# A four-layer hybrid transformer on one core: two of four weight pieces of the last feed-forward go from GpSimd to ScalarE and VectorE, the delta-net's key products move between the levels of its inverse, and the norms ask for their table earlier

## The reference

```python
def layer_norm(t, g, b):
    mu = jnp.mean(tf, -1, keepdims=True)
    var = jnp.mean(jnp.square(tf - mu), -1, keepdims=True)
    return ((tf - mu) * lax.rsqrt(var + NORM_EPS)).astype(t.dtype) * g + b

def conv_glu(t, w_up, conv_w, conv_b, w_down):       # D_FF = 2816
    hdn = t @ w_up
    val, gt = hdn[..., :D_FF], hdn[..., D_FF:]
    gt = dwconv(gt, conv_w) + conv_b
    return (jax.nn.silu(gt) * val) @ w_down

# gated delta-net: 8 heads, both directions, one chunk
tmat = triangular_solve(eye + lmat, eye)             # lmat from k k^T, beta and decay
def step(s, inp):
    v_new = uu - ww @ s
    o = qd @ s + aa @ v_new
    s = s * jnp.exp(gl)[..., None, None] + jnp.einsum('bhcd,bhce->bhde', kd, v_new)
    return s, o
# finish: rms_norm of o per head, times silu(gate), times w_o
```

## Time and profile before

| | us |
|---|---|
| median of 3 runs (2896.61 to 2898.7) | 2898.62 |
| the profiled execution, own time | 2901.96 |
| its span | 2899.9 |
| TensorE busy | 2652.6 (91%) |
| GpSimd busy | 1626.6 (56%) |
| VectorE busy | 1183.2 (41%) |
| ScalarE busy | 788.1 (27%) |

### The profile page before, as it was taken

The page is one execution under the profiler, slowest core; times in us unless marked ns, Lnnn a source line. Parts: engine busy times, 40 slices in busy tenths (PEclk is TensorE's granted clock), DMA queues, the critical chain, the costliest instruction groups (busy, mean ns, idle before and its releaser), DMA issues. The chain is left out here.

```text
span 2899.9 us, 45667 instructions
## 1 busy us (share of the span) xinstructions
PE 2652.6 (91%) x16461; PEld 2132.3 (74%) x16461; DVE 1183.2 (41%) x2197; ACT 788.1 (27%) x1490; POOL 1626.6 (56%) x1665
## 2 busy tenths in 40 slices
PE   6988999999898899899999999898999998888987
PEld 4766677787687788767778668886677786767886
DVE  2364322222469667432222320674322223443455
ACT  2253322210541433132211140441322113243311
POOL 3402566665657222466667556775666575607985
PEclk8999999999899989899999999999999999999998
DMA  6333455422222000255542222002555322203442
GB/s 236 117 117 117 155 172 173 151 87 87 61 73 87 16 2 1 73 173 173 173 132 87 73 76 88 16 1 89 188 174 174 116 88 72 88 1 116 159 145 87
DMA packets 217162, 305.60 MB, mean 105 GB/s; under 512 B 7332, under 2 KB 155551, under 8 KB 217024
## 3 DMA queue, kind: packets, MB, share of 16 engines
q1 hardware_dynamic: 179007, 228.16, 23.9%
q10 hardware_dynamic: 38016, 75.50, 8.0%
HBM read 302.60 MB, written 1.05 MB: 105 GB/s over the span
## 5 line engine op out<-in xcount | busy, mean ns | idle before, releaser
L588 POOL TENSOR_TENSOR w_lo<-w_raw,w_hi 128x512 fp32r<-128x512 f32 x720 | 948.5, 1317 | 108.2 <-POOL w_hi L585 88.1
L585 POOL TENSOR_SCALAR w_hi<-w_raw 128x512 fp32r<-128x512 f32 x720 | 472.1, 656 | 871.9 <-PE bank L1055 609.4
L1055 PE MATMUL bank<-u_lo,w_hi 128*128 128x512 f32 (+1 forms) x2144 | 810.3, 378 | 43.9 <-DVE u_lo L1725 21.5
L1055 PE MATMUL bank<-u_hi,w_lo 128*128 128x512 f32 (+1 forms) x2144 | 791.7, 369 | 0.0
L1055 PE MATMUL bank<-u_hi,w_hi 128*128 128x512 f32 (+1 forms) x2144 | 791.6, 369 | 0.0
L1055 PEld LDWEIGHTS bank<-u_lo,w_hi 128*128 128x128 f32 x2144 | 408.8, 191 | 182.9 <-issue 99.3
L1055 PEld LDWEIGHTS bank<-u_hi,w_hi 128*128 128x128 f32 x2144 | 408.7, 191 | 68.5
L1055 PEld LDWEIGHTS bank<-u_hi,w_lo 128*128 128x128 f32 x2144 | 409.4, 191 | 63.0
L1633 PE MATMUL bank<-gs_lo,w_hi 128*128 128x512 f32 (+1 forms) x576 | 212.2, 368 | 9.4 <-DVE gs_lo L2339 6.1
L1633 PE MATMUL bank<-gs_hi,w_lo 128*128 128x512 f32 (+1 forms) x576 | 211.1, 366 | 0.0
L1633 PE MATMUL bank<-gs_hi,w_hi 128*128 128x512 f32 (+1 forms) x576 | 211.1, 366 | 0.0
(11 more groups left out here) (334 smaller groups left out, 3859.6 us busy)
## 6 DMA issues: line engine op xcount, KB each, us to landing
w_raw<-in_ffn_w_up SPq DMA_DIRECT2D x88, 1024.0 KB, 7.1
ada_w<-in_ada_w ACTq DMA_DIRECT2D x72, 1024.0 KB, 5.2
w_raw<-in_ffn_w_down SPq DMA_DIRECT2D x44, 1024.0 KB, 4.9
ada_w<-in_ada_w SPq DMA_DIRECT2D x16, 1024.0 KB, 5.1
w_raw<-in_gdn_w_in SPq DMA_DIRECT2D x16, 1024.0 KB, 5.7
w_raw<-in_attn_w_qkv SPq DMA_DIRECT2D x12, 1024.0 KB, 5.3
w_raw<-in_gla_w_in SPq DMA_DIRECT2D x12, 1024.0 KB, 5.3
ada<-in_ada_w SPq DMA_DIRECT2D x8, 1024.0 KB, 13.5
```

The lines of the kernel that those rows point to most:

```text
L585: eng.tensor_scalar(w_hi[:, q, :], src, 1.0, 0.0, ALU.mult, ALU.add).then_inc(pool.own, pool.step())
L588: eng.tensor_tensor(w_lo[:, q, :], src, w_hi[:, q, :].bitcast(F32), ALU.subtract).then_inc(w_split, 1)
L1055: mm = eng.matmul(bank[banks[m]][:, T], w[:, q, c:c + P], v[:, k, T], start=(k == 0 and n == 0), stop=(k == KT - 1 and n == 2))
```

## The change

Three groups of edits.

1. Last feed-forward: GpSimd splits pieces 0 and 1 of a unit. Pieces 2 and 3 are rounded by ScalarE (`upper` on ScalarE) as soon as the same piece of the unit before has been multiplied, and VectorE subtracts (`upper` on VectorE). The release of a slot waits for 2 counts of `w_split` and 2 of `w_fourth`. The calls stand in fixed places of the in-order queues: on ScalarE ahead of the convolution's centre and ahead of silu.
2. Delta-net: the product of keys and state (`key_state`) is issued for d = 0 behind the first level of the inverse and for d = 1 behind the second; VectorE's residual values move behind its copies of the second level. In the two turns with s = 3 the transposed keys, decayed keys, state products and state updates are left out, as their result is not used. Waits follow.
3. Norms and finish: the one-column Sqrt (`root_table`) moves ahead of the wait for the means, and one is added at the head of `head_finish`, whose VectorE part gates four tiles before it inverts the root, and the others between the heads.

```diff
@@ load (SyncE)
-                    eng.wait_ge(w_split, sp.next(w_split, 3 if shared else 4))
+                    eng.wait_ge(w_split, sp.next(w_split, 2 if shared else 4))
                     sp.stand()
                     if shared:
-                        eng.wait_ge(w_fourth, sp.next(w_fourth))
+                        eng.wait_ge(w_fourth, sp.next(w_fourth, 2))
@@ delta_net (GpSimd)
-                        if (s, hg) != (0, 0):
+                        if (s, hg) == (TT - 1, 1):
+                            eng.wait_ge(od_ready, 14)
+                        elif (s, hg) != (0, 0):
                             eng.wait_ge(s_done, pool.next(s_done, 2))
@@ GpSimd, layers
-                pieces = 3 if last(l) else 4
+                pieces = 2 if last(l) else 4
@@ delta_net (ScalarE)
-                eng.wait_ge(s_done, act.next(s_done, 2))
-                eng.wait_ge(st_upd, act.next(st_upd))
+                eng.wait_ge(bo_ready, 16)
@@ head_finish, norm_stats (ScalarE)
+                root_table()
                 for i, t in enumerate(tiles):
...
+            def root_table():
+
+                eng.wait_ge(act.own, act.count())
+                eng.activation(warm[:], con[:, K_COL:K_COL + 1], ACT.Sqrt).then_inc(act.own, act.step())
+
             def norm_stats(l, w, ada_layer=None):
                 S = toks(l)
                 strips = slice(S.start // P * 32, P)
+                root_table()
                 eng.wait_ge(ms_ready, act.next(ms_ready))
...
-                eng.wait_ge(act.own, act.count())
-                eng.activation(warm[:], con[:, K_COL:K_COL + 1], ACT.Sqrt).then_inc(act.own, act.step())
                 eng.wait_ge(var_ready, act.next(var_ready))
@@ last feed-forward (ScalarE)
+                def upper(s, first=3):
+
+                    for q, n in ((2, first), (3, 1)):
+                        eng.wait_ge(w_done, act.next(w_done, n))
+                        act.stand()
+                        if q == 2:
+                            eng.wait_ge(w_loaded[s], act.next(w_loaded[s], 16))
+                            act.stand()
+                        eng.activation(w_hi[:, q, :], w_raw[:, s, q * PIECE:(q + 1) * PIECE], ACT.Copy).then_inc(w_round, 1)
+
                 def up_pair(i, load):
 
+                    if not more:
+                        upper((U + 1) % 2)
                     eng.wait_ge(g_done, act.next(g_done, 2))
...
+                    if not more:
+                        upper(U % 2)
                     for m in range(2):
                         eng.wait_ge(conv_done, act.next(conv_done))
...
-                    if wait:
+                    if wait and not more and slot % 2 == 1:
+                        upper((U + 1 + slot // 2) % 2, first=1)
+                    elif wait:
@@ delta_net (TensorE)
-                        if first:
-                            eng.wait_ge(st_upd, pe.next(st_upd))
-                        for d in range(2):
+                        def key_state(d):
+
+                            if first and d == 0:
+                                eng.wait_ge(st_upd, pe.next(st_upd))
                             if not first:
                                 eng.wait_ge(bo_ready, pe.next(bo_ready))
                             for b in range(4):
                                 mm = eng.matmul(bank[6 + d][:, C(b)], bk[:, H(b), tok[d]], bS[:, d, H(b), :], start=True, stop=True)
                             mm.then_inc(ks_ready, 1)
...
                             mm.then_inc(a_ready, 1)
+                        key_state(0)
...
                             mm.then_inc(b_ready, 1)
+                        key_state(1)
...
-                        for d in range(2):
+                        for d in range(2 if s < TT - 1 else 0):
                             for b in range(4):
                                 mm = eng.transpose(bank[3 * d + 1][:, C(b)], bk[:, H(b), tok[d]], ident)
...
                             mm.then_inc(od_ready, 1)
+                            if s == TT - 1:
+                                continue
@@ head_finish (VectorE)
+                gated(4)
                 eng.wait_ge(rt_ready, dve.next(rt_ready))
                 eng.reciprocal(srow[:], srow[:]).then_inc(hr_ready, 1)
-                eng.wait_ge(og_ready, dve.next(og_ready, KT))
                 for i in range(len(heads) + 1):
                     if i < len(heads):
                         eng.wait_ge(rb_ready, dve.next(rb_ready))
                         for t in heads[i]:
+                            eng.wait_ge(og_ready, dve.next(og_ready))
                             eng.tensor_tensor(o[:, t, :], o[:, t, :], bank[4 + i % 4][:], ALU.mult).then_inc(og2_ready, 1)
+                    if done[0] < KT:
+                        gated(len(heads[0]))
@@ last feed-forward (VectorE)
-            def fourth(s):
...
+            def upper(s):
+
+                for q in (2, 3):
+                    eng.wait_ge(w_round, dve.next(w_round))
+                    dve.stand()
+                    eng.tensor_tensor(w_lo[:, q, :], w_raw[:, s, q * PIECE:(q + 1) * PIECE], w_hi[:, q, :].bitcast(F32),
+                                      ALU.subtract).then_inc(w_fourth, 1)
+                dve.skip(w_done, 4)
...
-                        fourth((U + 1) % 2)
+                        upper((U + 1) % 2)
```

More of the change, by code:

```diff
@@ L823, in delta_net @@
                             Dm, E = bt[d][0:2]
-                            if not first:
+                            if (s, hg) == (TT - 1, 1):
+                                eng.wait_ge(od_ready, 14)
+                            elif not first:
                                 eng.wait_ge(s_done, act.next(s_done))
@@ L974, in _ @@
                 make_u(l, 1, l, l + 1 if more else None)
+                U = unit_of_up
+                if not more:
+                    for n in range(U + 1):
+                        act.skip(w_loaded[n % 2], 16)
+                def upper(s, first=3):
[6 more added lines that the diff above has]
+                        eng.activation(w_hi[:, q, :], w_raw[:, s, q * PIECE:(q + 1) * PIECE], ACT.Copy).then_inc(w_round, 1)
                 def up_pair(i, load):
+                    if not more:
+                        upper((U + 1) % 2)
                     eng.wait_ge(g_done, act.next(g_done, 2))
                     act.stand()
-                    eng.wait_ge(w_done, act.next(w_done, 4))
-                    act.stand()
+                    if more:
+                        eng.wait_ge(w_done, act.next(w_done, 4))
+                        act.stand()
                     for m in range(2):
@@ L1020, in _ @@
                 act.skip(g_done, -2)
-                with act.loop(4, {w_done: 8}) as i:
+                with act.loop(4, {w_done: 8} if more else {w_done: 8, w_loaded[0]: 16, w_loaded[1]: 16}) as i:
                     for j in range(4):
@@ L1025, in _ @@
                     g_hi(f % 4, g[:, f, T], True)
-                act.skip(w_done, 8)
+                if not more:
+                    upper(U % 2)
+                act.skip(w_done, 8 if more else 4)
                 norm_stats(l, 1)
@@ L1037, in piece @@
             def piece(q, shared):
-                if shared and q == 3:
+                if shared and q >= 2:
                     eng.wait_ge(w_fourth, pe.next(w_fourth))
@@ L1368, in delta_net @@
                         for d in range(2):
-                            if not first:
+                            if not first and (s, hg) != (TT - 1, 1):
                                 eng.wait_ge(st_upd, pe.next(st_upd))
@@ L1611, in _ @@
                 up_pair(0, u_tile)
-                pieces = {w_split: 6, w_fourth: 2} if last(l) else {w_split: 8}
+                pieces = {w_split: 4, w_fourth: 4} if last(l) else {w_split: 8}
                 per = {**pieces, conv_done: 2, g_done: 2}
@@ L2193, in head_finish, with gated @@
             def head_finish(o, gate, heads, nw):
-                for h in heads:
-                    for m, t in enumerate(h):
+                tiles = [(m, t) for h in heads for m, t in enumerate(h)]
+                done = [0]
+                def gated(n):
+                    for m, t in tiles[done[0]:done[0] + n]:
                         eng.wait_ge(hs_ready, dve.next(hs_ready))
@@ L2296, in _ @@
                 if not more:
-                    for n in range(U + 1):
-                        dve.skip(w_loaded[n % 2], 16)
-                    per = {**per, own["dve"]: 4, w_loaded[0]: 16, w_loaded[1]: 16}
+                    per = {**per, w_round: 4}
                 if more:
@@ L2326, in up_pair @@
                     else:
-                        fourth(U % 2)
+                        upper(U % 2)
                     for m in range(2):
@@ L2353, in _ @@
                 if not more:
-                    per = {**per, w_done: 8, own["dve"]: 2, w_loaded[0]: 16, w_loaded[1]: 16}
+                    per = {**per, w_done: 8, w_round: 4}
```

(10 more changed lines are left out.)

49 lines of the change are left out of this document (23 added, 26 removed).

## The result

The changed kernel takes 2824.16 us (median of 4, 2821.01 to 2826.77) beside 2898.66 of the kernel before (2896.61 to 2902.93): the ratio is 0.9741, 95% interval 0.9724 to 0.9758, a gain of 74.5 us. The forecast was 2836, a gain of 62.2, with a range of 2817 to 2855. The time lies in the range and is that of the second rival, 2824: the sum, and the clock of the delta-net on top. A second set on another chip gave 2824.31, ratio 0.9745 (0.9731 to 0.9758).

What follows compares the result with a forecast made beforehand. GpSimd was taken to bound the last feed-forward, and a chain from engine to engine the delta-net. Gains of 34.9 + 16.1 + 4.5 + 1.2 + 5.5 = 62.2 us gave 2836 us, range 2817 to 2855.

Steps and rivals of the forecast that it cites:

- second rival: Delta-net: key products fill TensorE's gaps, so its granted clock rises too, 12 us beyond the sum; 2824 us, chance 0.2.
- Feed-forward, 34.9 forecast: Last feed-forward: units fall from 6.57 to TensorE's 5.76 us, gaining 32.0 with stalls counted; the last unit gains 2.9.
- The stalls: Last feed-forward, TensorE: 0.9 us at the second piece, then 0.3, 1.4 and 0.4 at the first, second and last down-unit.
- The convolution's room, 0.6: Last feed-forward: rounding piece 3 ahead of the convolution makes 5.2 us, under the value unit's 5.76, leaving 0.6.
- Third rival, loads: Last feed-forward: loads landing in 7.1 us instead of 5.15 bind, costing 12 us; 2848 us, chance 0.14.
- Fourth rival, the port: Last feed-forward: each VectorE subtraction holds up GpSimd for its whole length, so GpSimd stays the bound; 2849 us, chance 0.12.
- Delta-net, 16.1: Delta-net turns: gain from the new order, omitted transposes and omitted state products together, 16.1 us; lower bound 6.5.
- Order 9.6: Delta-net: inverse levels start earlier without key-state products ahead of them, 1.2 us a turn, 9.6 for eight.
- Transposes and state products 6.5: Delta-net turns with s = 3: omitted transposes save 2 x 1.9 us, omitted state products 2.7.
- Finishes: Ends of delta-net and linear attention: earlier inversion brings the factor's rows sooner, gaining 4.5 and 1.2 us; range 0 to 8.
- Norms: Norms: root 0.1 us behind the sums, saving 1.0 in two narrow and 0.9 in four wide ones, 5.5 us.
- Fifth rival: Last feed-forward: exposed hand-off through ScalarE and VectorE makes a unit 8.3 us and the kernel slower, 2924 us, chance 0.03.

Runs made afterwards that it cites:

- the delta-net alone: The kernel before with only the delta-net's edits (key-state products between the levels, work for the unused last state left out): 2873.76 us, ratio 0.9915.
- the order alone: The kernel before with only the delta-net's new order, all transposes and state products kept: 2872.49 us, ratio 0.991.
- three copies per piece: The changed kernel with two extra ScalarE copies ahead of each rounding of `upper`, into a tile nobody reads there: 2843.51 us, ratio 0.982.
- the norms alone: The kernel before with only the norms' one-column Sqrt moved ahead of the wait for the means: 2891.32 us, ratio 0.998.

## Why the prediction held, and its steps

Part by part the traces give 33.8 us for the 34.9 forecast in the feed-forward, 28.3 for 16.1 in the delta-net's turns, 7.7 for 5.7 in the two finishes and some 4 for 5.5 in the norms, 73.8 for 62.2. So the sum was short by one part, the delta-net, and the range holds the result because it took in the second rival.

**Feed-forward, 34.9 forecast.** The traces give 34.8 with the last norm's 1.0 in it, so 33.8; from the norm ahead to the last down-unit 30.9 of 32.0, behind it 3.8 of 3.9 (last unit and norm). The unit of 5.76 is right to the hundredth, GpSimd's 4.5 us per unit are 4.4 (4.0 busy, the 70%, and 0.4 of waits on itself), and three pieces bring nearly the old time back. The stalls were put too low: 0.3, 1.4 and 0.4 at the first, second and last down-unit, where TensorE is idle for 0.69, 2.44 (1.50 and 0.94) and 0.92 us.

**The convolution's room, 0.6.** Right in effect, wrong in its parts: the table load left the chain, as it stands ahead of the rounding that TensorE's third piece releases, and the loop's turn of 0.77 entered it. The measured room is about 0.4, and 1.06 us more on ScalarE costs 0.64 per pair. The kernel stands that near to a worse result.

**Third rival, loads.** The landing is 7.0 us by the profile's median and 5.98 in the chain. GpSimd waits for loads 9 times in the up-units, 14.7 us in all, at most 1.7 at a time, and no unit of TensorE is late there. At the first down-unit one is: GpSimd waits 1.5 us for the load of the chain shown above, TensorE 0.69 for GpSimd. In this the rival saw the next limit.

**Fourth rival, the port.** The Trainium skill, "SBUF — State Buffer", section "Who interferes with whom", has VectorE and GpSimd hold the port in turns, the whole of an instruction each. The prediction found the rule "not seen in full". These traces show it in full. In the changed kernel a GpSimd subtraction and a VectorE subtraction that starts 0.02 us behind it:

```profile
2782.84 1.30 POOL L589 TENSOR_TENSOR w_lo<-w_raw,w_hi 128x512 fp32r<-128x512 f32 x1 [0.18 <-POOL w_hi L586]
2782.86 1.82 DVE L2268 TENSOR_TENSOR w_lo<-w_raw,w_hi 128x512 fp32r<-128x512 f32 x1 [0.68 <-ACT w_hi L997]
```

VectorE's takes 0.69 us alone, 1.82 here, and ends 0.55 behind GpSimd's. Of its 64 subtractions 24 start during one of GpSimd's; 23 of these end 545 to 552 ns behind it, wherever in it they started, which is what waiting for its end gives. The other way round it holds too: in the kernel before, VectorE's subtraction of 0.87 still runs for 0.35 us when GpSimd's begins, and GpSimd's takes 1.49 for 1.29. The rival had the mechanism and mis-sized its price. It let GpSimd pay for the whole of each VectorE subtraction, but whoever comes second pays, and at most for what is left of the first. Here that is mostly VectorE (mean 0.96 for 0.69), which has the time; GpSimd's subtraction is 1.32 on the mean and its rounding 0.72 for 0.63. Where VectorE hasn't the time it shows: the last down-unit waits 0.92 us for a `w_lo` of 1.39.

**Delta-net, 16.1 and the clock's 12.** The step that failed is the clock's place in the sum: it was made a rival with 0.2, and it is the largest part of the delta-net's gain. Order 9.6: 8.7 measured at full clock. Clock 12: 18.8 against the trace of before, since seven turns ran below full clock and not six, since two of them, the fourth and the eighth, ran at 0.80 and took 25.5 us, of which the prediction had read neither, and since it took 1.8 off for the transposes. Transposes and state products 6.5: 4.0 at full clock. The transposes were priced from a row at half clock, 1.97 us in the earlier trace rows; in the turn of before that ran at 1.00 the same eight take 1.10:

```profile
1090.64 1.10 PE L1427 MATMUL bank<-con,bk 128*128 128x128 f32 x8
```

So this term holds some 1.7 us (2 x 0.87) that belong to the clock. The errors cancel, by luck: 28.1 was forecast with the clock, 28.3 stands in the trace of the delta-net alone, made of 8.7, 18.8 and 2.6, less some 2 for its first turn, which ran at 0.91 (22.92 us, 20.77 in the order alone).

**Finishes.** Delta-net 4.5 forecast: from the last output's addition to the next norm four traces with the old finish and the state update take 79.0 us on the mean, the changed kernel 74.2, so 4.8. With the finish alone changed it is 74.7, 4.3, where the prediction's terms without the state update make 3.2. Linear attention 1.2 forecast: from the last output to the projection's start 17.6 us became 14.7, so 2.9; the whole layer gives 3.0 on the means of all traces, the norm's 0.5 in it, and 3.7 between the two of before and after. The loss of 2.1 ahead of the first low part did come due: the projection starts 8.0 us behind the rows of the factor (1928.61 to 1936.61), where it started 6.0 behind them. What failed is the 1.5 charged for the table load, which runs at 1902.68, under the last outputs; the rows come 4.9 us earlier, not 3.4. **Norms**, 5.5: the last one gained its 1.0, the wide ones 0.5 each where 0.9 were forecast (there the root stood only 0.7 behind the sums), some 4 in all.

**Fifth rival.** It decided from 7.45 us per unit on. The hand-off is covered by the two GpSimd pieces that TensorE multiplies meanwhile, 2.9 us; even with three copies per piece the unit was 6.75.

## What to carry to other kernels

A stage that is short of one engine gains only down to the next need in line, so work out that need first: here TensorE's 5.76 us, and it was met exactly. Where the turns of a loop run at different granted clocks, price the same turn at both and put the better one into the sum as its own term, because 1.1 us less per turn brought 2.3 us more by the clock. Read all turns of a loop for that, not three, and look at the clock of each row that gives a price. Where two engines hold each other up, ask which comes second: it pays, and at most for what is left of the other. And when something is put ahead of a covered chain, list the loop's own turn with the chain: 0.77 us of it decided over the room.

## What the runs showed of the hardware

- The same 250 matmuls with the same waits took 21.82 us at a granted clock of 1.00, 24.1 at 0.86 and 25.5 at 0.80. A slowest turn is followed by the fastest in the kernel before (25.54, then 21.82) and in the norms alone (25.49, then 21.82). TensorE is busy 90% of the fast turn, 93% to 94% of the slow ones, and 97% of the new order's second to sixth turn, which run at 1.00 in every trace; its first and eighth turn fall to 0.91 to 0.93 in some. What decides between them the runs don't show.
- VectorE's subtraction with both inputs in SBUF that starts during one of GpSimd's ends 0.55 us behind it in 23 of 24 cases of the changed kernel, so the second of the two waits for the first; alone it takes 0.69.
- Two traces of one code differ by up to 4.6 us between the norms around the delta-net (483.0 to 487.6), and ahead of the first norm by 5 us: a single trace prices an edit of 2 us only locally.
- A table load needs no time beside its 1.28 us: in the finish, after 9.5 us of idle, the load starts at 1140.16 and the next ScalarE instruction at 1141.46; right behind a rounding that ends at 2660.74 it starts at 2660.76 and the next instruction at 2662.05.
- In the changed kernel the load of ScalarE's table stands ahead of a plain copy (L997, x9 in the stage), while in the kernel before it stood ahead of the convolution's first instruction (L984 in the earlier trace rows): both are the first instruction of ScalarE behind the Silu of the pair before.
